# Exponentials two units ahead and scores directly behind the values in differential attention

## The reference

```python
for start in range(0, s_len, blk):
    end = start + blk
    mask = kpos[None, :] <= qpos[:, None]
    z1 = einsum('bhqd,bhkd->bhqk', q1[:, :, start:end], k1[:, :, :end]) * scale
    z2 = einsum('bhqd,bhkd->bhqk', q2[:, :, start:end], k2[:, :, :end]) * scale
    p1 = softmax(where(mask, z1, -inf)); p2 = softmax(where(mask, z2, -inf))
    w = p1 - lam * p2
    outs.append(einsum('bhqk,bhkd->bhqd', w, v[:, :, :end]))
```

## Time and profile before

| | |
|---|---|
| median of three runs | 1520.76 us |
| the profiled execution, its own time | 1519.07 us |
| its span in the trace | 1516.9 us |
| PE matmul busy | 1475.1 us (97%) |
| PE weight load busy | 1226.8 us (81%) |
| VectorE busy | 1007.9 us (66%) |
| ScalarE busy | 666.8 us (44%) |
| GpSimd busy | 328.2 us (22%) |
| mean granted PE clock | 0.994 of full speed |
| differential groups in the trace | about 430 to 677 us |

### The profile page before, as it was taken

One profiled execution on the slowest core, in us unless ns is written; L12 is line 12 of the kernel. 1 busy time (PEld: TensorE's weight loads), 2 busy tenths in 40 slices (PEclk: granted clock), 3 DMA queues, 4 the chain that ended last, 5 costly groups with the idle time before them and its releaser, 6 DMA issues. The chain is left out here.

```text
span 1516.9 us, 19312 instructions
## 1 busy us (share of the span) xinstructions
PE 1475.1 (97%) x7152; PEld 1226.8 (81%) x7152; DVE 1007.9 (66%) x1232; ACT 666.8 (44%) x1035; POOL 328.2 (22%) x212
## 2 busy tenths in 40 slices
PE   8999999999999998999999999999999999999997
PEld 7788888887887787888787877888888888888886
DVE  3677877779866556553346688766665467668767
ACT  3455554546556555443021344444444344433343
POOL 2535444446432223210130140000000000000004
PEclk9999999999999999998999999999999999999999
DMA  5101112111110000110452233644442677935553
GB/s 177 56 29 57 56 43 70 55 55 56 43 57 28 29 14 28 39 48 12 136 183 107 89 110 116 217 153 153 153 153 97 215 275 256 325 137 194 194 196 137
DMA packets 111503, 172.40 MB, mean 114 GB/s; under 512 B 6080, under 2 KB 71616, under 8 KB 111296
## 3 DMA queue, kind: packets, MB, share of 16 engines
q1 hardware_dynamic: 111424, 171.33, 33.2%
HBM read 127.27 MB, written 44.04 MB: 113 GB/s over the span
## 5 line engine op out<-in xcount | busy, mean ns | idle before, releaser
L756 PE MATMUL p_proj<-xt_h,w_hi 128*128 128x512 f32 x640 | 254.6, 398 | 0.2 <-DVE xt_l L1589 0.2
L760 PE MATMUL p_proj<-xt_h,w_lo 128*128 128x512 f32 x640 | 253.5, 396 | 0.0
L758 PE MATMUL p_proj<-xt_l,w_hi 128*128 128x512 f32 x640 | 252.1, 394 | 0.0
L2265 POOL TENSOR_TENSOR w_lo<-w_raw,w_hi 128x1024 fp32r<-128x1024 f32 x48 | 120.4, 2508 | 240.2 <-DVE w_hi L1596 239.7
L760 PEld LDWEIGHTS p_proj<-xt_h,w_lo 128*128 128x128 f32 x640 | 120.8, 189 | 23.6
L756 PEld LDWEIGHTS p_proj<-xt_h,w_hi 128*128 128x128 f32 x640 | 120.8, 189 | 22.4 <-DVE xt_l L1589 0.6
L758 PEld LDWEIGHTS p_proj<-xt_l,w_hi 128*128 128x128 f32 x640 | 120.9, 189 | 20.7
L2378 POOL TENSOR_TENSOR row_odd<-row_odd,gains 128x1024 f32<-128x1024 f32 x4 | 10.4, 2622 | 580.7 <-ACT row_odd L1561 580.7
L1589 DVE TENSOR_TENSOR d_al<-f_a,d_ah 128x1024 fp32r<-128x1024 f32 x56 | 68.5, 1224 | 79.5 <-ACT d_ah L1479 79.5
L1479 ACT ACTIVATE d_ah<-f_a 128x1024 fp32r<-128x1024 f32 x56 | 59.2, 1057 | 134.0 <-PE p_av L1130 54.9
L1328 ACT ACTIVATE a_t<-p_tr 128x384 fp32r<-128x384 f32 (+3 forms) x96 | 47.2, 491 | 123.4 <-PE p_tr L858 123.3
(11 more groups left out here) (287 smaller groups left out, 3537.1 us busy)
## 6 DMA issues: line engine op xcount, KB each, us to landing
f_a<-h_terms SPq DMA_DIRECT2D x56, 512.0 KB, 3.4
w_raw<-w_in SPq DMA_DIRECT2D x40, 512.0 KB, 3.9
h_terms<-c SPq DMA_DIRECT2D x40, 512.0 KB, 3.2
f_b<-w_ff SPq DMA_DIRECT2D x40, 512.0 KB, 4.9
r<-w_ff SPq DMA_DIRECT2D x32, 512.0 KB, 4.0
gate_rows<-gst SPq DMA_DIRECT2D x12, 512.0 KB, 5.0
y<-x SPq DMA_DIRECT2D x8, 512.0 KB, 7.8
wo_raw<-w_out SPq DMA_DIRECT2D x8, 512.0 KB, 8.8
```

What stands on the lines that cost most here:

```text
L756: pe.matmul(o, w_hi[n_slot][:, k, :], xt_h[:, k, cols], start=(k == 0), stop=False)
L758: pe.matmul(o, w_hi[n_slot][:, k, :], xt_l[:, k, cols], start=False, stop=False)
L760: mm = pe.matmul(o, w_lo[n_slot][:, k, :], xt_h[:, k, cols], start=False, stop=(k == KT - 1))
L2265: pool.tensor_tensor(w_lo[slot][:, :, :], w_raw[:, :, :], w_hi[slot][:, :, :].bitcast(F32), ALU.subtract).then_inc(wt_lo, 1)
```

## The change

On PE, a one-batch unit no longer issues two thirds of its filler before the scores: the scores come directly behind the values and all filler of the batch behind them. On ScalarE, the list `scored` is gone: the exponentials of unit u+2 are issued in batch k of unit u itself, m = 0 in its first batch and m = 1 in its last, behind `out_up` and ahead of the stacks and of the copies of finished halves. They wait for the peaks of the same batch. `project_done` is renamed and takes one half at a time; its content is as before. VectorE, GpSimd and the DMA queue are not edited.

```diff
@@ attention on PE
                     elif u + 2 < G.nunits:
-                        if b == 0 and last_b:
-                            before = G.until[k - 1] if k else G.head
-                            fill_to(before + (G.until[k] - before) * 2 // 3)
                         if b == 0:
                             scores(g, 2 * u + 4, True)
                         if last_b:
@@ attention on ScalarE
-                def project_done(k):
-                    for i in ([0] if k < 0 else G.halves_at(k)):
-                        t, h = i // 2, i % 2
+                def project_half(i):
+                    t, h = i // 2, i % 2
...
-                project_done(-1)
-                scored = []
+                project_half(0)
                 for k, (u, b) in enumerate(G.batches):
...
-                    else:
-
-                        while scored:
-                            exponentials(*scored.pop(0))
-                        if u + 2 < G.nunits:
-                            scored += [(u + 2, 0)] * (b == 0) + [(u + 2, 1)] * last_b
+                    if not G.sb and u + 2 < G.nunits:
+                        if b == 0:
+                            exponentials(u + 2, 0)
+                        if last_b:
+                            exponentials(u + 2, 1)
                     if G.last and 8 <= k < 11:
                         square(k - 8)
                     if stack_part(G, k) is not None:
                         stacks(g + 1, G.rope, stack_part(G, k))
-                    project_done(k)
+                    for i in G.halves_at(k):
+                        project_half(i)
```

More of the change, by code:

```diff
@@ new lines, in project_half, with free @@
+                def project_half(i):
+                    t, h = i // 2, i % 2
+                    if G.is_rope(t):
+                        act.wait_ge(pj_done, G.tile(t) * 2 + (h + 1))
+                        if not (isinstance(g, int) and g == SB_GROUPS - 1 and i == 0):
+                            act.wait_ge(rp_done, G.roped(t, h))
+                        for qd in range(4):
+                            mm = act.activation(swap[32 * qd:32 * qd + 32, :],
+                                                p_proj[32 * (qd ^ 1):32 * (qd ^ 1) + 32, h, :], ACT.Copy)
+                        mm.then_inc(rp_swap, 1)
+                    else:
+                        def free():
+                            if G.last and t == 2:
+                                act.wait_ge(s_gst, 16 * 10)
+                            elif t == 2:
+                                act.wait_ge(tr_done, G.tr(2))
+                            else:
+                                act.wait_ge(st_act, g * 4 + 4)
+                                act.wait_ge(st_dve, g * 4 + 4)
+                                act.wait_ge(st_pool, g * 2 + 2)
+                        if t >= 3:
+                            gate_half(t, h)
+                        else:
+                            plain(G.tile(t), h, gst[0] if G.last and t == 2 else stage[t], free)
```

## The result

| | before | changed |
|---|---|---|
| median of five runs, us | 1520.76 | 1527.79 |
| lowest to highest | 1519.68 to 1521.26 | 1526.24 to 1528.31 |
| profiled execution, us | 1519.07 | 1527.54 |
| its span | 1516.9 | 1525.5 |
| PE matmul busy | 1475.1 | 1478.3 |

The changed kernel is slower: the ratio is 1.0045 with a 95% interval of 1.0034 to 1.0057, or 7.0 us between the medians and 8.5 us between the two profiled executions.

The account below looks back on a forecast made before the run. TensorE, busy 1475.1 of 1516.9 us, was taken as the bound. Three groups at +3.0, group 7 at -1.3 and clock +1.5 gave +9.2 on 1519.07, or 1528.3; plus 1.7 profile-to-median, 1530.0 us; range 1517.5 to 1540.

Parts of the forecast that it names:

- What the change removes: Groups 4 to 6: 2.6 us of TensorE idle time a group goes, about 3.1 us with the hidden part.
- A, B and C: Group 4 TensorE waits for exponentials before scores of units 3, 5, 6: 0.86, 0.41, 1.31 us; all to vanish.
- Unit 1: Group 4: swaps 1.1 us late behind an exponential; transposes of unit 2 stand until 451.4; lag +0.65 us.
- Unit 3: GpSimd holds unit 3's combination to 456.2 (lower bound 455.1); half 2's swaps 3.1 us late; lag at unit 4 +2.1.
- Units 4 and 5: Scores of unit 6 wait 0.6 us; half 3's swaps 2.9 us late; copy of transposes lets TensorE on 2.0 later.
- D: TensorE's wait for the combination at unit 6's transposes, 1.96 us in group 4: ends 2.9 us late, becomes about 3 us.
- the bound that I gave for handshakes: Groups 4 to 6, 3.0 us longer each: upper bound 3.6 us, allowing 0.6 us for missed handshakes.
- Group 7: Group without rotary halves: only a 1.31 us wait for an exponential goes; -1.3 us, bounds 0 and -2.0.
- Clock: One more fall of TensorE's clock behind the lengthened wait at unit 6's transposes: +1.5 us, bounds -1.5 to +6.
- the wait at unit 4 that I named as a sign: Groups 4 to 6: a wait at the transposes of unit 4 for the combination would show the mechanism; sign without size.
- rival 1: Faster, the rotary chain has slack in groups 4 to 6: 1510 us, or 1503 us if D goes too; chance 0.19.
- Rival 2: Peaks on VectorE are late so exponentials hardly move, or gain and loss cancel: 1518 to 1524 us; chance 0.11.

Follow-up runs that it names:

- run 1: Kernel before with only the TensorE part of the change (scores directly behind the values, exponentials one unit ahead as before): 1545.62 us, ratio 1.0158.
- run 10: Changed kernel with three VectorE moves (combination a batch earlier, rotary sum behind combination and peaks, cosine product one batch later): 1501.79 us, ratio 0.9874.
- runs 3 and 4: Changed kernel with rotary swap copies ahead of the exponentials again: 1520.96 us; kernel before with half 3's swap copies made twice in groups 4 to 6: 1526.89 us.
- run 9: Changed kernel with the combination of unit u+1 issued in the first batch of two-batch units, not the last: 1524.93 us, ratio 1.0027.
- 5 and 6: VectorE's weight cast, and with it GpSimd's subtraction, one batch later: on the changed kernel 1526.57 us, on the kernel before 1521.72 us.
- runs 5, 6 and 8: Late weight cast on the changed kernel (1526.57 us), on the kernel before (1521.72 us), and on the changed kernel together with a late rotary sum (1520.33 us).

## Why the prediction was right

The forecast was 1530.0 us and slower; it is 1527.8 us, slower by 0.45%.

Lag is how much later than before PE is at a place, counted from the start of the group.

**What the change removes.** As predicted: A, B and C are gone in the changed kernel, and run 1 shows what stands there without the early exponentials.

**Unit 1.** Predicted: swaps 1.1 us late, transposes of unit 2 waiting 1.65 us, lag 0.65. Measured: 1.3, 1.75 and 0.9. **Unit 3.** Predicted: combination about 2.3 us long, swaps of half 2 3.1 us late, lag at unit 4 2.1. Measured: 2.17, 3.4 and 2.5. The upper bound, which I took for the hold, was right. The Trainium skill (page "SBUF — State Buffer", section "SBUF: two separate sides") has a VectorE operation with two SBUF inputs and a GpSimd one take an exclusive lock, and the one that comes second fully blocks. The traces agree: the 512-wide combination takes 0.75 us without GpSimd at work, and it ended 0.54 us behind GpSimd's end when it had met 0.6 us of it (kernel before) and 0.55 us behind when it had met 1.6 us (changed) or 2.07 us (run 10). A shared bandwidth would have made that rest shorter the longer they overlap. **Units 4 and 5.** Predicted: 0.6 us at the scores of unit 6, swaps of half 3 2.9 us late, copy's wait 0.7 (the lag grows from 1.3 to 2.0). Measured: 0.39, 3.35 and 0.64. **D.** Predicted 2.9 us late and a wait near 3; measured 3.3 to 3.4 late and 2.8 to 2.9 long.

The size that was off is the time between two instructions on ScalarE. I let swaps start 1.0 us behind the start of a 1.01 us exponential; they started 1.12 us behind it (472.56 to 473.68), and with 0.11 to 0.12 us at each of the three such places the swaps of half 3 are 0.35 of their 0.45 us later than I had them. The other 0.1 us I can't place. All lies inside the bound that I gave for handshakes.

**Group 7.** Predicted -1.3, measured -1.5 us. **Clock.** One fall more behind D, predicted and measured, at 1.5 us. That this term came out is luck: the fall of group 5 went and two others came, in groups 4 and 6, and I had no reason for one rather than none or three. A window granted 0.62 is also not half of its time at 1.2 GHz, as I wrote, but three quarters of it; the loss of 1.5 us is right. Not foreseen were two more falls, behind the waits of units 2 and 4 in groups 4 (0.75 and 0.82 granted from 452 to 460 us) and 6 (0.89 and 0.68 from 584 to 592 us); they cost nothing, because the lag at the transposes of unit 4 is 2.5 us in group 4, 2.6 in group 6, and 2.6 in group 5 as well, which had no such fall: PE waited 1.45 us there for the combination, and where the clock fell it came as late by itself. So the wait at unit 4 that I named as a sign shows in group 5 alone. **The ends.** 0.4 us ahead of the groups and -1.9 us behind them were no part of the sum. They, and a gap between profile and median that was 1.7 us before and 0.25 us after, take the forecast from 1530 to 1527.8. The three long groups were 1.1 us more than forecast, so part of the closeness is errors that cancel; the mechanism, place by place, is not.

**The rivals.** The slack that rival 1 needed is refuted by runs 3 and 4. Rival 2 (exponentials hardly move) is refuted by the trace, in which A, B and C are gone, and by run 1, which is 18 us worse without them. What I hadn't seen is that a gain of the size of rival 1 lay behind VectorE's order: run 10 has 1501.8 us, and the upper case of rival 1 was 1503. That these two numbers are so close is chance, since run 10 changes VectorE too.

## What to carry to other kernels

Making an engine's result earlier can be worth nothing until its consumer's place in the program order moves too: here the change cost 7 us by itself, and with the combination, the rotary sum and the cosine product moved on VectorE the whole is 19 us faster than before. Before such a 19 us is put down to the first change, run the second one without it; that run is missing here. When an instruction that waits is moved ahead of one that was ready, add up what the ready one feeds, through every engine, before counting the wait that goes. And single moves that win little or only shift a wait to the next late step (2.9 us in run 9, 1.2 us and nothing in 5 and 6) don't show that several together are worthless.

## What the runs showed of the hardware

A VectorE operation that reads two SBUF tensors stands nearly still while GpSimd subtracts: the 896-wide combination takes 1.15 us alone and 2.97 us across GpSimd, the 512-wide one 0.75 and 2.17 to 2.62, and the last one 1.28 and 2.2 to 2.8. Whether the 512-wide one meets 0.45 or 2.07 us of the subtraction, it ends 0.54 to 0.56 us behind it in every run, and the 896-wide one 0.93 to 0.96 us. A cast with one SBUF input is held too: the two of the keys take 1.40 us, and 3.50 across the subtraction (runs 5, 6 and 8). The peaks of unit 7, which read PSUM, are not: 1.22 us inside the subtraction (run 10) and 1.21 outside (changed kernel).

A wait of 1.75 to 2.9 us on TensorE brings a stretch at 1.2 GHz in some groups and not in others. Before, D had none behind 1.96 us in group 4 and 2.06 us in group 6, and one behind 2.06 us in group 5. In the changed kernel it had one behind 2.81 and 2.90 us in groups 4 and 6 and none behind 2.89 us in group 5, and the waits at unit 2 had one behind 1.75 and 1.93 us (groups 4 and 6) and none behind 1.91 us (group 5). Half speed cost about 1.5 us each time it met no other wait.
